# MLP down-projections of six stretches as seven block products over a summed residual basis

## The reference

```
hm = _rmsnorm(x, g_mlp)
x  = x + jnp.square(jax.nn.relu(hm @ w_up)) @ w_down      # 1024 -> 4096 -> 1024
y  = _rmsnorm(x, g_final)
```

## Time and profile before

| | us |
|---|---|
| median of three runs (lowest, highest) | 2250.39 (2249.12, 2258.05) |
| the profiled execution's own time | 2245.91 |
| its span, first to last instruction | 2244.1 |
| PE busy, share of the span | 2182.6, 97% |
| DVE busy | 1065.8, 47% |
| ACT busy | 533.4, 24% |
| POOL busy | 440.1, 20% |

### The profile page before, as it was taken

One profiled execution on the slowest core, in us unless ns is written; L12 is line 12 of the kernel. 1 busy time (PEld: TensorE's weight loads), 2 busy tenths in 40 slices (PEclk: granted clock), 3 DMA queues, 4 the chain that ended last, 5 costly groups with the idle time before them and its releaser, 6 DMA issues. The chain is left out here.

```text
span 2244.1 us, 49247 instructions
## 1 busy us (share of the span) xinstructions
PE 2182.6 (97%) x21418; PEld 2061.6 (92%) x21418; DVE 1065.8 (47%) x1526; ACT 533.4 (24%) x1014; POOL 440.1 (20%) x368
## 2 busy tenths in 40 slices
PE   8999999999999999999999999998999999999997
PEld 6899888888888899989999987998999999999997
DVE  5333643636445355263544155466445445354455
ACT  4111433324333221153011023231102011011023
POOL 0233301112021022122333200321111111111110
PEclk9999999999999999999999999999999999999999
DMA  8446513424053074336113125111212122122122
GB/s 306 144 129 137 142 39 82 89 54 149 7 114 70 27 244 162 105 135 254 47 40 119 47 96 187 38 57 62 70 53 76 57 67 72 52 76 64 55 76 80
DMA packets 86663, 217.61 MB, mean 97 GB/s; under 512 B 10720, under 2 KB 26464, under 8 KB 83680
## 3 DMA queue, kind: packets, MB, share of 16 engines
q1 hardware_dynamic: 62944, 156.22, 21.0%
q0 software_dynamic: 12800, 33.56, 6.9%
q10 hardware_dynamic: 10752, 25.35, 3.2%
HBM read 187.04 MB, written 61.60 MB: 111 GB/s over the span
## 5 line engine op out<-in xcount | busy, mean ns | idle before, releaser
L517 PE MATMUL ps<-A_s,w_split 128*128 128x364 f32 (+1 forms) x3888 | 693.5, 334 | 1.9 <-ACT zstg L2250 1.9
L517 PEld LDWEIGHTS ps<-A_s,w_split 128*128 128x128 f32 x3888 | 643.5, 188 | 28.1 <-issue 12.5
L517 PE MATMUL ps<-hid,msp 128*128 128x364 f32 (+3 forms) x2304 | 388.3, 330 | 5.4 <-issue 5.4
L517 PEld LDWEIGHTS ps<-hid,msp 128*128 128x128 f32 x2304 | 385.1, 189 | 7.3 <-issue 6.0
L449 POOL CAST w_split<-w_raw 128x1024 fp32r<-128x1024 f32 x78 | 85.5, 1096 | 1117.0 <-PE ps L517 858.0
L517 PE MATMUL ps<-B_s,w_split 128*128 128x364 f32 (+1 forms) x1728 | 288.1, 328 | 0.4 <-POOL w_split L451 0.4
L517 PEld LDWEIGHTS ps<-B_s,w_split 128*128 128x128 f32 x1728 | 286.7, 188 | 0.7 <-issue 0.7
L1434 DVE TENSOR_TENSOR F<-ps,F 128x1092 f32<-128x1092 f32 (+3 forms) x84 | 104.3, 1241 | 352.3 <-PE ps L517 352.3
L509 POOL CAST msp<-mraw 128x512 fp32r<-128x512 f32 x176 | 115.1, 655 | 616.6 <-PE ps L517 604.0
L451 POOL TENSOR_TENSOR w_split<-w_raw,w_split 128x1024 fp32r<-128x1024 f32 x78 | 206.9, 2652 | 6.3
L517 PE MATMUL ps<-xb,msp 128*128 128x272 f32 x1536 | 200.2, 288 | 1.5 <-DVE F L1434 1.5
(11 more groups left out here) (249 smaller groups left out, 2408.4 us busy)
## 6 DMA issues: line engine op xcount, KB each, us to landing
w_raw<-w SPq DMA_DIRECT2D x80, 512.0 KB, 3.7
mraw<-w SPq DMA_DIRECT2D x112, 256.0 KB, 2.6
sums_up<-w POOLq DMA_DIRECT2D x24, 1024.0 KB, 9.4
mraw<-sums_up SPq DMA_DIRECT2D x64, 256.0 KB, 2.6
z<-zstg SPq DMA_DIRECT2D x83, 182.0 KB, 2.1
F<-z SPq DMA_DIRECT2D x16, 546.0 KB, 7.1
sums_up<-sums_up POOLq DMA_DIRECT2D x8, 1024.0 KB, 5.9
w_raw<-w SPq DMA_DIRECT2D x7, 1024.0 KB, 10.3
```

The source lines that it names most:

```text
L517: return pe.matmul(out, lhsT, rhs, start=start, stop=stop, skip_group_check=skip)
```

## The change

The down-projection of six stretches (all but the first and the last) is done as seven block products too. The blocks are: hidden features of the even or the odd quad, even or odd output tiles, first or second half of the tokens. A product is two weight units; a unit holds two output tiles of two k each, so 24 matmuls of 272 columns, and TensorE signals the first tile of a unit (`m_half`) and the second (`m_used`) on their own. A stretch has 14 units in place of 8. The four sums of weight blocks come from a new DRAM tensor, `sums_down`, built by POOL in the steps after the splits 32, 33, 34 and 41 to 69; the loops of POOL's splits are written out for that. The sums of hidden blocks are made by DVE, partly in a new buffer `tf`, with ACT rounding them (`turned_hi`) and DVE making their low parts (`turned_lo`, `lower`). The even quad no longer makes low parts, the odd quad two. DVE reads each product once per tile (544 columns), 28 reads in a stretch. So that one read suffices, two blocks of the residual hold sums with a third one (`residual_in` after the quad (0, 2), and back after the quad (3, 2)). In the opening the low parts are made in another order, and the first down-projection starts when two of them are there, one k at a time over both tiles. The middle accumulator of the quads moves from PSUM banks 3 and 4 to 2 and 3.

```diff
+        FAST = [(p, u) for p in (1, 2, 7, 3, 5, 4, 6) for u in range(2)]
+        def mlp_fast(o, d):
+            return (o, d) not in ((0, 0), (3, 1))
...
+            def plus(g, dst, src):
+                parts = [(dst[:, d], src[:, d]) for d in range(2)] if len(dst.shape) == 4 else [(dst, src)]
+                for x, y in parts:
+                    pool.dma_start(x, y, accum_op=ALU.add).then_inc(d_sum[g], 16)
...
+            for n in range(XT + SIDE + S_CQ - S_MIX):
                 split(n, n % 2)
                 if n < 32:
-                    sum_step(n)
+                    sum_step(n, 0, sum_block, up_block)
+                elif n < 35:
+                    sum_step(n - 32, 8, down_sum, down_block)
+                elif n >= 41:
+                    sum_step(n - 41 + 3, 8, down_sum, down_block)
...
@@ TensorE
+            def down_first():
+                r = [mlp_ring(0, down_unit(0, 0, t)) for t in range(2)]
                 for t in range(2):
-                        pe.wait_ge(m_lo, BEFORE + 7)
-                        pe.wait_ge(m_b, BEFORE + 5 + t)
+                    pe.wait_ge(m_ready, mlp_units(0, 0, down_unit(0, 0, t) + 1))
+                    pe.wait_ge(m_lo, mlp_lows(0, 0, 0, 2))
+                    pe.wait_ge(m_b, BEFORE + 5 + t)
+                    down_part(r[t], t, (0,))
+                for k, n in ((2, 4), (1, 6), (3, 8)):
+                    pe.wait_ge(m_lo, mlp_lows(0, 0, 0, n))
+                    for t in range(2):
+                        last = down_part(r[t], t, (k,))
...
+            OPERAND = {1: (0, 0), 2: (1, 0), 7: (0, 1), 3: (1, 1), 5: (0, 0), 4: (1, 0), 6: (0, 0)}
+            NEED = {1: 1, 2: 3, 7: 4, 3: 6, 5: 5, 4: 7, 6: 8}
+            def down_fast(i, o, d):
+                n = 4 * o + 2 * d + 2
+                for s, (p, u) in enumerate(FAST):
+                    l = down_unit(o, d, s)
+                    v, h = OPERAND[p]
+                    if u == 0:
+                        pe.wait_ge(m_lo, mlp_lows(i, o, d, NEED[p]))
+                    pe.wait_ge(m_ready, mlp_units(i, o, l + 1))
+                    for j in range(2):
+                        t = 2 * u + j
+                        if s >= 2:
+                            pe.wait_ge(m_f, mlp_reads(i, o, d, 4 * (s // 2 - 1) + t + 1))
...
+                        for k in range(2):
+                            for m, (wp, xp) in enumerate(((0, 0), (0, 1), (1, 0))):
+                                for c in range(2):
+                                    x0 = HT * h + HC * c
+                                    last = mm(ps[:, 2 * t + c, 0:HC], msp[:, mlp_ring(o, l), wp, 2 * j + k, :], hid[v][:, k, xp, x0:x0 + HC],
+                                              start=(p in (1, 7, 5, 6) and k == m == 0), stop=(k == 1 and m == 2), skip=p in (2, 3, 4))
+                        last.then_inc((m_half, m_used)[j], 1)
@@ VectorE, quad
+                if odd:
+                    squares_of(i, z0)
+                    own.add(tt(tf, H11, H12, ALU.subtract))
                 unit_lo(i, o, l0 + 7)
                 c.c22()
-                hidden_lo(i, z0, q, 0, 0)
+                if alone:
+                    hidden_lo(i, z0, q, 0, 0)
+                if odd:
+                    own.wait()
+                    lower(0, 0)
...
                 unit_lo(i, o, l0 + 9)
+                if odd:
+                    squares_of(i, z0 + 3)
+                    tt(H12, H12, H22, ALU.subtract).then_inc(t_sum, 1)
                 c.c21()
...
                 unit_lo(i, o, l0 + 10)
-                hidden_lo(i, z0 + 3, q, 1, 0)
+                if alone or odd:
+                    hidden_lo(i, z0 + 3, q, 1, 0)
@@ VectorE, down
+            def down_fast(i, o, d):
+                for s, (p, u) in enumerate(FAST):
+                    l = down_unit(o, d, s)
+                    v.wait_ge(m_half, mlp_turns(i, o, d, 14, BEFORE + s + 1))
+                    read(p, 2 * u)
+                    v.wait_ge(m_used, mlp_units(i, o, l + 1))
+                    read(p, 2 * u + 1)
+                    unit_lo(i, o, l + 4)
+                    if s == 0:
+                        turned_lo(H12, 0, 1, mlp_turns(i, o, d, 4, BEFORE_R + 5))
+                    if s == 2:
+                        turned_lo(tf, 0, 0, mlp_turns(i, o, d, 4, BEFORE_R + 6))
+                        v.wait_ge(m_lo, mlp_lows(i, o, d, 5))
+                        own.add(tt(tf, H22, tf, ALU.add))
+                    if s == 3:
+                        own.wait()
+                        lower(1, 1)
+                        own.add(tt(H21_hi, f32(hid[1][:, :, 0, 0:HT]), tf, ALU.subtract))
+                    if s == 4:
+                        own.wait()
+                        tt(H21, H21_hi, f32(hid[1][:, :, 1, 0:HT]), ALU.add).then_inc(t_sum, 1)
+                    if s == 6:
+                        turned_lo(H21, 1, 0, mlp_turns(i, o, d, 4, BEFORE_R + 7))
+                    if s == 10:
+                        turned_lo(tf, 0, 0, mlp_turns(i, o, d, 4, BEFORE_R + 8))
...
+            def residual_in(n, op1, op2):
+                v.wait_ge(m_f, n)
+                own.add(tt(F12, F12, F22, op1))
+                own.add(tt(F21, F21, F22, op2))
+                own.wait()
@@ ScalarE
+            def down_fast(i, o, d):
+                a.wait_ge(t_sum, mlp_turns(i, o, d, 2, BEFORE + 4))
+                turned_hi(0, 1, hidf[0][:, :, 1, HT:T])
+                a.wait_ge(m_used, mlp_units(i, o, down_unit(o, d, 1) + 1))
+                turned_hi(0, 0, tf)
+                a.wait_ge(t_sum, mlp_turns(i, o, d, 2, BEFORE + 5))
+                turned_hi(1, 0, hidf[1][:, :, 1, 0:HT])
+                a.wait_ge(m_used, mlp_units(i, o, down_unit(o, d, FAST.index((5, 1))) + 1))
+                turned_hi(0, 0, tf)
```

## The result

| | before | after |
|---|---|---|
| median of nine runs each (lowest, highest), us | 2250.7 (2248.77, 2258.05) | 2258.04 (2254.12, 2263.93) |
| ratio, 95% interval | | 1.0032 [1.0019, 1.0046] |
| the profiled execution's own time, its span, us | 2245.91, 2244.1 | 2263.93, 2261.7 |

The changed kernel is 0.3% slower. By the bound of 0.5% that is no change, but it lies 32 us above the forecast of 2225.5 and outside the range.

A forecast was written before the change was run, and what follows sets the result against it. PE's matmul time was taken as the bound, with DVE having cover. The terms -34.4 + 12 - 5.1 + 2.5 = -25.0 us against the median 2250.4 gave 2225.5 us, with an 8-in-10 range of 2212 to 2241.

The forecast's parts named there:

- The sums in DRAM: Puts and pluses on POOL: issuing them costs PE nothing, their transfers 2.5 us, in the gate stage.
- Rival 3: Weight slots at 1080 and 1160 run full, late weights cost 10 us more: 2235 us; chance 0.12.
- step 9 in the gate stage: Half a MB issued at about 1020, ahead of a late split: 2.5 us taken, 0 to 3.3, up to 6.
- The matmuls removed: Six down stretches: 14 units of 3.012 us, 42.17 in place of 47.91, saving 34.4 us if PE never waits.
- DVE's waits: PE waits for DVE's F in the six changed stretches: 2.0 us each, 12 us in all, between 0 and 25.
- the casts: POOL's casts beside DVE in a changed stretch: three cost DVE 0.4 us each, raising PE's waits to 2.3 us.
- the layout: DVE's order of operations laid out over a changed stretch: PE waits about 1.2 us at s=6, before casts.
- The opening: First down-projection: starts 2.4 us earlier and the clock stays full, saving 2.7 more: 5.1 us, bounds 2 and 5.5.
- 1 (DVE bounds): DVE bounds the changed stretches, with PE waits of 4.2 us in each: 2238.6 us; chance 0.16.
- 2 (no waits): PE never waits for DVE in the changed stretches: -38.5 us, 2212 us; chance 0.13.
- Rival 4: A PE wait over 4.5 us at s=6 drops the clock in each changed stretch: 2266 us; chance 0.04.
- late weight slots between 1000 and 1300 us: Weight slots ahead of the MLP stage: their coming late was named as showing the prediction wrong.

The follow-up runs named there:

- experiment 1: The changed kernel without the transfers that build sums_down, its units reading as many bytes of sums_up instead: 2229.47 us, ratio 0.9909.
- experiment 2: The kernel before with only the transfers that build sums_down added, nothing reading the result: 2283.84 us, ratio 1.0137.
- experiment 4: The changed kernel with the put behind split 34 moved to split 41 and all later steps one split on: 2252.12 us, ratio 1.0002.
- experiments 7 and 9: DVE's wide operations spread over the changed stretch, with transfers in POOL's long idle gaps (2268.09 us) or one behind a split (2216.23 us).
- experiment 5: The changed kernel with each of the two pluses of a pair accumulating 384 rows rather than 512: 2244.03 us, ratio 0.9981.
- experiment 6: The changed kernel with 28 of the 32 steps for sums_down issued in POOL's long idle gaps: 2280.41 us, ratio 1.0114.
- experiment 8: The changed kernel with its 40 transfers for sums_down issued one behind a split, the last eight in the first MLP stage: 2227.13 us, ratio 0.989.

## Why the prediction was wrong

**The sums in DRAM: the step that failed.** The prediction gave POOL "at most 2.6 + 0.7 us behind a split that has 7 us of idle time behind it: nothing for PE". POOL is held until the transfer before has landed, some 8 us, and the term that stood at +2.5 us costs 28.6 (experiment 1) to 35.0 (experiment 2). Three things were wrong in it.
- I counted POOL's issue of a plus at 1.26 us each and two in a row at 2.5. In the kernel before a plus never follows another closely, so those rows hold no price for the second one. It was a case for a bound. The page of before has the transfers of 1 MB from w, two thirds of them pluses, land after 9.4 us. If each half of a pair takes as long, two take 18.8 us in a slot of 11.95, 6.9 us short in each of eight slots with a pair: 55 us; if time goes by bytes, the two take 9.4 and nothing is short. With both ends kept, a slower result would have been in the range. Measured, a half takes 8.3 us to land, near the dear end; that no more than 28.6 of the 55 us came is because four of the eight slots cost PE nothing.
- I took the cost of a transfer from the share of the DMA engines and called the slots after 1056 free since bytes had room. Bytes were not the limit: half a MB and a MB in the same 512 rows land after 8.3 and 9.7 us, and from 1068 to 1135 us the DMA engines are busy for 68% of the time. Rival 3 named these slots and late weights; but it had the DMA engines full, at 12.6 us of all of them for a MB, where eight half pluses take 54.6% of those 67 us, 4.6 us each, 9.1 a MB. It priced the loss at 10 us.
- The put behind split 34 was in no term. It is worth about 6 us (experiment 4), and PE's waits for zstg, behind writes on which ACT waits, are what fell with it.

The place that I did price, step 9 in the gate stage, was right in kind: PE waits 3.56 us for the split behind it, where it was 0.39 in the earlier trace rows. That is 3.2 us for the 2.5 taken. The some 1.6 us at the lower clock behind it I had not counted; 4.8 lies within my bound of 6.

**The matmuls removed: right.** Between the waits a unit takes 3.01 to 3.06 us, small gaps included (the eight from 1692.28 on take 24.34 us), and 14 of them make the stretch but for the waits.

**DVE's waits: right in kind and place, a little small.** With the casts the layout has 2.3 us, 1.0 of them at s=5; the trace has 0.96 at s=5 and 1.26 at s=6, in all 2.46 with the small gaps, where I took 2.0. Over six stretches that is 14.8 against 12. That the cause is wide operations standing together, not DVE's total, experiments 7 and 9 show: the same operations in another order leave 0.7 us. On the lock of the SBUF port, the Trainium skill (page SBUF — State Buffer, section Who interferes with whom) let me count a cast only against operations with two inputs in SBUF; with three casts at 0.4 us the layout comes within 0.2 us of the trace. The stretch itself agrees: its 28 reads of F, with one input in SBUF, take 0.71 to 0.72 us beside a cast and without one, while the low part at 1681.47, beside the cast at 1681.40, takes 1.08 us and others 0.68. At times it is the cast that loses: the one at 1684.46 takes 1.63 us. No run here took the casts away.

**The opening: 3.4 us, not 5.1.** This is a second step that failed, at 1.7 us. PE's idle time fell to 3.45 us as the layout said (3.6). But the granted clock fell all the same. Windows after, with PE alone, answer to the earlier trace rows:

```profile
1578.00:1580.00 2.00, 0.00 (x0) 1.00 0.00 0
1580.00:1582.00 2.00, 1.93 (x9) 0.73 0.35 124
1582.00:1584.00 2.00, 2.00 (x8) 0.50 0.46 138
1584.00:1586.00 2.00, 2.00 (x12) 0.91 0.65 204
```

I had argued from one row in which the clock was still full after 4.2 us of idle time. Here it was still full when PE started again at 1580.08 too, and fell less than 1 us later (0.73 is the mean of the window): a full clock at the end of a wait doesn't show that the wait is free. The kernel of experiment 4, with the same idle time of 3.45 us, kept it:

```profile
1570.00:1572.00 2.00, 1.51 (x9) 1.00 0.16 50
1572.00:1574.00 2.00, 2.00 (x14) 1.00 0.59 210
```

Of the nine kernels with this opening, one profiled execution each, eight fell to 0.50 and experiment 4's did not; its first down stretch takes 48.2 us, the others 49.7 to 50.8. The same idle time gives either, so one row decides nothing here. With the clock kept, the opening gained 5.0 us, as I had forecast (5.1).

**The rest.** -34.4 + 14.8 - 3.4 = -23.0, and the MLP stage gained 22.4; the missing 0.6 is a longer wait at the turn of the loop (2.04 us against 1.48). In the two profiled executions the part ahead of the MLP stage also holds 6.2 us that are there without any transfer (experiment 1's first MLP matmul starts at 1495.95, that of before at 1489.79); one execution each, so I make nothing of it. Without the price of the transfers the forecast would be 2223.0; experiment 1 measured 2229.5. Of these 6.5 us, 2.8 are DVE and 1.7 the opening, and 2 stay open.

**Rivals.** 1 (DVE bounds), 2 (no waits) and 4 (the clock falls in each stretch) did not come: a stretch's waits are 2.46 us and PE's pace in them stays near 3.01 us. Rival 3 had the place and a third of the price, by another mechanism, and the prediction named late weight slots between 1000 and 1300 us as a sign of being wrong: that sign came. My only rival on the side of a loss sat in the MLP stage, since I looked for trouble where the matmuls were changed. Rival 4 also took it that the clock falls only behind a wait of over 4.5 us; in the weight slots it fell behind 2.58.

## What to carry to other kernels

When a change adds a transfer to an engine's queue directly behind another, take the landing time of the first as the upper bound for the issue of the second, and ask what stands behind it on that engine: here a 3 us split that PE needed every 11.95 us. Take that landing time from the place where the transfer will stand: beside the gate stage's loads it was 15 to 19 us, elsewhere 8. Room is counted per slot and per queue, in time to landing, not in bytes. If such work can be cut up, one piece in each slot hides what two in each of four slots in a row do not: 2227 against 2258 us for the same transfers.

## What the runs showed of the hardware

- An accumulating transfer DRAM to DRAM of 512 rows lands after 8.3 us with 1 KB rows (median of 24, the longest 18.9), 9.7 with 2 KB rows (of 16). A second one directly behind it holds GpSimd's instruction stream until the first has landed, some 6.8 us (all 17 held ones come 0.26 to 0.38 us after that landing); with 384 rows each two are issued within 2.5 us, and a third waits until both have landed (experiment 5). The Trainium skill (page DMA: Bandwidth & Descriptors, section SWDGE vs HWDGE vs iDMA) has GpSimd append descriptors to rings that the DMA engines drain. A hold that depends on the number of rows agrees with a full ring; that the third of 384 rows waits for both before it is not explained by that. The page names no depth, and no run here measured one.
- Transfers from GpSimd's queue in stretches of many small matmuls went with 41 us of waits of PE for which the profile shows no releaser, 5.6 the longest (experiment 6), while one transfer in each stretch of large matmuls cost none (experiment 8).
- The same idle time of PE, 3.45 us, was followed by a granted clock of 0.50 in eight kernels and of 1.00 in one. Behind the five waits for w_split, 2.58 to 6.94 us, it fell to 0.50 each time, and the slot behind lost about 1.6 us more.
